# The scores of even and odd dilated heads, issued together on the two row halves of TensorE

## The reference, cut to what matters

```python
s = jnp.einsum('gnqhd,gnkhd->gnhqk', qs, kk).astype(jnp.float32) * (dh ** -0.5)
s = jnp.where(valid[None, :, None], s, NEG)
m = jnp.max(s, axis=-1, keepdims=True)
e = jnp.exp(s - m)
den = jnp.sum(e, axis=-1, keepdims=True)
o = jnp.einsum('gnhqk,gnkhd->gnqhd', (e / den).astype(v.dtype), vv)
```

## Time and profile before

| | |
|---|---|
| median of 3 runs | 2309.15 us (2308.07 to 2310.26) |
| the profiled execution | 2309.35 us, span of its instructions 2308.0 us |
| block two | from about 1300 us to the end |
| the two attention loops | about 1481 to 1529 us, and 2018 to 2063 us |

### The profile page before, as it was taken

The page is one execution under the profiler, slowest core; times in us unless marked ns, Lnnn a source line. Parts: engine busy times, 40 slices in busy tenths (PEclk is TensorE's granted clock), DMA queues, the critical chain, the costliest instruction groups (busy, mean ns, idle before and its releaser), DMA issues.

```text
span 2308.0 us, 28941 instructions
## 1 busy us (share of the span) xinstructions
PE 1955.2 (85%) x12336; PEld 1357.2 (59%) x12336; DVE 983.3 (43%) x1219; ACT 669.7 (29%) x812; POOL 66.9 (3%) x144
## 2 busy tenths in 40 slices
PE   7999999655666655666679999999999999999998
PEld 4768872111111111111136999779998999788997
DVE  3744661000000000000005657876658656876656
ACT  3433430000000000000004445564445444455444
POOL 0000000000000000000001001010001000100000
PEclk8999999778777787877799999999999999999999
DMA  7345899999999999999997554335554554424552
GB/s 307 120 173 206 321 371 426 429 433 429 433 430 432 431 431 429 433 428 433 429 405 297 192 206 153 133 137 183 192 183 164 190 194 174 152 90 176 195 193 87
DMA packets 53489, 647.44 MB, mean 281 GB/s; under 512 B 5936, under 2 KB 6448, under 8 KB 10096
## 3 DMA queue, kind: packets, MB, share of 16 engines
q1 hardware_dynamic: 53360, 645.59, 69.9%
HBM read 644.52 MB, written 1.05 MB: 280 GB/s over the span
## 4 chain that ended last, share of the span: by engine, by line
PE 59%; DMA 30%; DVE 6%; ACT 2%; issue 1%; POOL 1%; SPq 0%; DVEq 0%; ACTq 0%; POOLq 0%
DMA wide_b<-in_experts 29%; PE PS L490 14%; PE PS L492 13%; PE PS L491 13%; PE PS L948 4%; PE PS L983 4%; DVE low L1887 1%; PE PS L508 1%; PE PS L739 1%; PE PS L926 1%; PE PS L642 1%; PE PS L756 1%; PE PS L1260 1%; DMA ring<-in_wmod 1%; DVE XR L1951 1%
## 5 line engine op out<-in xcount | busy, mean ns | idle before, releaser
L1887 DVE TENSOR_TENSOR low<-ring,WH 128x2048 fp32r<-128x2048 f32 (+1 forms) x163 | 372.0, 2282 | 182.0 <-ACT WH L2276 179.4
L490 PE MATMUL PS<-XH,WH 128*128 128x256 f32 x1408 | 396.9, 282 | 3.2 <-DVE XL L1919 3.1
L491 PE MATMUL PS<-XL,WH 128*128 128x256 f32 x1408 | 395.2, 281 | 0.0
L492 PE MATMUL PS<-XH,low 128*128 128x256 f32 x1408 | 393.1, 279 | 0.0
L2276 ACT ACTIVATE WH<-ring 128x2048 fp32r<-128x2048 f32 (+1 forms) x164 | 313.1, 1909 | 28.1 <-PE PS L983 16.5
L490 PEld LDWEIGHTS PS<-XH,WH 128*128 128x128 f32 x1408 | 264.5, 188 | 6.7 <-issue 5.0
L492 PEld LDWEIGHTS PS<-XH,low 128*128 128x128 f32 x1408 | 267.4, 190 | 0.0
L491 PEld LDWEIGHTS PS<-XL,WH 128*128 128x128 f32 x1408 | 264.6, 188 | 1.4
L1869 DVE TENSOR_TENSOR T1S<-T1S,PS 128x512 f32<-128x512 f32 x16 | 11.0, 688 | 546.6 <-PE PS L948 546.6
L948 PE MATMUL PS<-ring,big 128*32 128x512 f32 x936 | 137.9, 740 | 52.3 <-DMA ring<-in_experts 52.3
L2544 ACT ACTIVATE T1S<-PS 128x512 f32<-128x512 f32 x16 | 9.6, 597 | 539.9 <-PE PS L948 539.9
(11 more groups left out here) (445 smaller groups left out, 2845.6 us busy)
## 6 DMA issues: line engine op xcount, KB each, us to landing
wide_b<-in_experts SPq DMA_DIRECT2D x30, 4096.0 KB, 23.7
wide_a<-in_experts SPq DMA_DIRECT2D x29, 4096.0 KB, 23.7
ring<-in_experts SPq DMA_DIRECT2D x28, 4096.0 KB, 24.0
ring<-in_fg SPq DMA_DIRECT2D x44, 1024.0 KB, 4.9
ring<-in_fu SPq DMA_DIRECT2D x44, 1024.0 KB, 4.9
ring<-in_fd SPq DMA_DIRECT2D x44, 1024.0 KB, 4.8
ring<-in_wmod SPq DMA_DIRECT2D x24, 1024.0 KB, 6.6
ring<-in_wgt SPq DMA_DIRECT2D x12, 1024.0 KB, 9.1
```

The costliest lines, as they stand in the source:

```text
L490: t.matmul(o, l[0], r[0], start=start, stop=False, skip_group_check=True)
L491: t.matmul(o, l[0], r[1], start=False, stop=False, skip_group_check=True)
L492: return t.matmul(o, l[1], r[0], start=False, stop=stop, skip_group_check=True)
L1887: own(v.tensor_tensor(low[:, w.slot.index, 0:size], w.flat, WH[:, w.slot.index, 0:size].bitcast(f32), ALU.subtract).then_inc(*c.wl.up()), ...
```

## The change

The six dilated groups of a layer are issued as three pairs by a new function `dilated_scores(g)`: it takes both score banks, and issues the matmuls of the even head (rows 0 to 63 of the array, bank 0) and of the odd head (rows 64 to 127, bank 1) in turn, head for head. So that the two groups of a pair hold neighbouring heads, the list of groups for the second 128 queries goes from heads (0, 2), (4, 6), (1, 3), (5, 7) to (0, 2), (1, 3), (4, 6), (5, 7). The pairs stand in steps 5, 7 and 9 of TensorE's loop; before, the six groups stood in steps 4 to 9. The programs of the other engines keep their text.

```diff
         groups = [(hs, m, 512 // len(hs), o) for o in (4, 6)
-                  for hs, m in [([0, 2, 4, 6], 0), ([1, 3, 5, 7], 0)] + [([h, h + 2], 1) for h in (0, 4, 1, 5)]]
+                  for hs, m in [([0, 2, 4, 6], 0), ([1, 3, 5, 7], 0)] + [([h, h + 2], 1) for h in (0, 1, 4, 5)]]
...
-                    if g == 6:
-                        P.wait_ge(c.dqv, 2 * l + 2)
-                        P.wait_ge(c.dqa, 2 * l + 2)
                     for i, h in enumerate(hs):
-                        if g < 6:
-                            q, k = QT2[0:96, h, m * 128:m * 128 + 128], KT[0:96, h, 0:w]
-                        else:
-                            s = slice(64 * (h % 2), 64 * (h % 2) + 64)
-                            q, k = DT[s, 0, h // 2, m * 128:m * 128 + 128], DT[s, 1, h // 2, 0:w]
-                        x = t.matmul(PS[:, b, i * w:i * w + w], q, k, start=True, stop=True)
+                        x = t.matmul(PS[:, b, i * w:i * w + w], QT2[0:96, h, m * 128:m * 128 + 128], KT[0:96, h, 0:w],
+                                     start=True, stop=True)
...
+                def dilated_scores(g):
+
+                    m, w = groups[g][1:3]
+                    take(0)
+                    take(1)
+                    if g == 6:
+                        P.wait_ge(c.dqv, 2 * l + 2)
+                        P.wait_ge(c.dqa, 2 * l + 2)
+                    n = len(groups[g][0])
+                    for i in range(n):
+                        for b in range(2):
+                            h = groups[g + b][0][i]
+                            s = slice(64 * b, 64 * b + 64)
+                            x = t.matmul(PS[:, b, i * w:i * w + w], DT[s, 0, h // 2, m * 128:m * 128 + 128],
+                                         DT[s, 1, h // 2, 0:w], start=True, stop=True)
+                            if i == n - 1:
+                                x.then_inc(*c.sc.up())
+                                held[b] = [(c.am, 12 * l + g + b + 1)]
...
                 for g in range(13):
-                    if g < 10:
+                    if g < 4:
                         scores(g + 2)
+                    if g in (5, 7, 9):
+                        dilated_scores(g + 1)
```

More of the change, by code:

```diff
@@ L1227, in scores @@
                         P.wait_ge(c.qta, 4 * l + 8)
+                    for i, h in enumerate(hs):
+                        x = t.matmul(PS[:, b, i * w:i * w + w], QT2[0:96, h, m * 128:m * 128 + 128], KT[0:96, h, 0:w],
+                                     start=True, stop=True)
+                    x.then_inc(*c.sc.up())
+                    held[b] = [(c.am, 12 * l + g + 1)]
+                def dilated_scores(g):
+                    m, w = groups[g][1:3]
+                    take(0)
+                    take(1)
                     if g == 6:
@@ L1230, in scores @@
                         P.wait_ge(c.dqa, 2 * l + 2)
-                    for i, h in enumerate(hs):
-                        if g < 6:
-                            q, k = QT2[0:96, h, m * 128:m * 128 + 128], KT[0:96, h, 0:w]
-                        else:
-                            s = slice(64 * (h % 2), 64 * (h % 2) + 64)
-                            q, k = DT[s, 0, h // 2, m * 128:m * 128 + 128], DT[s, 1, h // 2, 0:w]
-                        x = t.matmul(PS[:, b, i * w:i * w + w], q, k, start=True, stop=True)
-                    x.then_inc(*c.sc.up())
-                    held[b] = [(c.am, 12 * l + g + 1)]
+                    n = len(groups[g][0])
[6 more added lines that the diff above has]
+                            if i == n - 1:
+                                x.then_inc(*c.sc.up())
+                                held[b] = [(c.am, 12 * l + g + b + 1)]
                 def turns(g):
```

## The result

The change makes the kernel slower: 2336.36 us (median of 4, 2333.74 to 2338.05) against 2308.61 us for the kernel before; ratio 1.0117, 95% interval 1.0105 to 1.0129. That is 27 us. Run once more beside other kernels it was 1.0113 (1.0098 to 1.0128), 26 us.

The account below looks back on a forecast made before the run. TensorE is busiest, but VectorE's in-order queue, with under 5 us of slack, was taken to bound the loop once pairs come late. 2309.2 us + 18.0 for waits + 3 for the clock = 2330 us; range 2318 to 2341.

Parts of the forecast that it names:

- Steps 4 and 6 save nothing: TensorE's loop: `values(3)` and `values(5)` wait for VectorE's copies with or without scores issued ahead, so nothing is saved.
- The price of a pair: TensorE, steps 5, 7 and 9: 1.9 us for width 128, 1.3 us for width 256; bounds one burst to about two.
- full overlap: Case of row halves running wholly side by side: about 8.0 us lost a layer, 16 us for both.
- The rival that the halves don't overlap: Pairs in the loop: 10.4 us lost a layer, 2330 us, up to 2338 with clock loss; chance 0.86 together with the forecast.
- The walk: Step-by-step sum of delays through steps 5 to 11 of the loop: 9.0 us lost a layer, 18.0 for both.
- The clock: TensorE's granted clock falling behind its standstills: 1.5 us a layer, 3 us for both, bounds 0 to 8.
- first standstill: TensorE in step 6, before `values(5)`, waiting for VectorE's copy of `turns(5)`: about 4 us.
- second standstill: TensorE in step 7, before the first slice of `w_out`, waiting for VectorE's `low_rows`: over 2 us.
- last standstill: TensorE in step 10, before `values(9)`, waiting for VectorE's copy of `turns(9)`: some 3 us.
- Only the first standstill counts: Rival: ScalarE or VectorE catches up in steps 7 to 9, leaving 2.6 us a layer, 2314 us; chance 0.07.
- TensorE's saving shows: Rival: VectorE's copy is not late, so saved TensorE time shows: 2.5 up to 6.6 us, 2303 to 2307 us; chance 0.04.
- No change: Rival: VectorE's late steps and the saved matmuls cancel within 4.6 us; chance 0.03.

Follow-up runs that it names:

- late, kept apart: Changed kernel with each pair's even group first, one unused full-height identity matmul, then the odd group: 2336.07 us, ratio 1.0115.
- The fillings: Changed kernel with unused identity matmuls at the three standstills of TensorE in each layer: 2326.38 us, ratio 1.0079.
- the first set of runs: The changed kernel's first runs against the kernel before: 2336.36 us, ratio 1.0117; its second set, on another chip, gave 2333.96 us, ratio 1.0113.
- the last pair alone: Changed kernel with only the pair of groups 10 and 11 late (step 9), the others in steps 4 and 6: 2316.61 us, ratio 1.0033.
- early pairs and changed queues: Changed kernel with pairs in steps 4, 6 and 8 and work in VectorE's and ScalarE's queues reordered: 2303.53 us, ratio 0.9979.
- the early pairs: Changed kernel with the pairs issued one step earlier, in steps 4, 6 and 8: 2309.18 us, ratio 1.0008.
- the early pairs issued one group after the other: Changed kernel with pairs in steps 4, 6 and 8, all matmuls of one group before the other's: 2311.12 us, ratio 1.0014.
- only the first standstill filled: Changed kernel with 16 unused identity matmuls ahead of `values(5)` only: 2327.93 us, ratio 1.0086.

## Why the prediction was right, point by point

- **The direction and the place: right.** 2330 us was forecast, 2336 measured, inside the range of 2318 to 2341. VectorE idles 4.22 us before `masked(6)`, where over 4 were forecast; TensorE 4.08 before `values(5)` (some 4), 2.37 in step 7 (over 2), 2.90 before `values(9)` (some 3). That VectorE's order is the cause is shown by changing that order alone (half of the loss gone) and by moving the pairs back a step (all of it gone).
- **Steps 4 and 6 save nothing: right.** `values(3)` still starts 1.45 us behind the start of `turns(3)`, now with a wait of 0.85 us for the copy. Before it was 1.62, so a little, 0.2 us, was saved.
- **The price of a pair: mis-sized.** The prediction took 1.9 us for width 128, on the assumption that weight loads go one after the other, and 1.3 for width 256. Measured at full clock: 1.16 and 1.14 us, the price of one burst; the row halves overlap wholly, loads included. The first choice was the wrong end of its range. It put `masked(6)` 0.7 us too late; by the prediction's own bound for full overlap the waits are 16 us, not 18. The rival that the halves don't overlap is out, by these times and by "late, kept apart".
- **The walk: right.** It gives 8.0 us a layer for full overlap. With the clock held up by filling, the loops are 7.9 us longer in each layer. The medians, with 18.5 us for both, are coarser: their interval is 14.8 to 21.7.
- **The clock: mis-sized.** It was taken at 3 us, with bounds of 0 and 8. The fillings show 7.6 us by the medians, and in the traces the two loops are longer than with the fillings by 8.5 us (profile of the first set of runs) and 6.6 (of the second). The term counted only the 2.8 us of work behind the first standstill, and that at half its price. In windows of the trace PEclk is 0.50 from 1508 us on, through the second standstill, and 1.00 again from 1522 us. Beside the kernel with the fillings, layer one loses 2.2 us from `values(5)` to the first slice of `w_out`, where 1.4 were taken, and 2.5 from there to the pair of step 9, where nothing was: there `values(6)` and `turns(7)` take 1.80 and 1.06 us, and slices of `w_out` 0.63 instead of 0.39. The prediction put that stretch at nothing without giving a reason. A third fall behind the last standstill (PEclk 0.83 from 1530 to 1540 us) was foreseen as small.
- **Luck.** The two errors, 2 us too much for the pairs and some 4 to 5 too little for the clock, partly cancel; part of the nearness of 2330 to 2336 is owed to that.
- **The rivals.** "Only the first standstill counts": out, since the last pair alone costs 8.6 us. "TensorE's saving shows": out for this placing. It is real in the kernel with early pairs and changed queues, at 3.5 us for six pairs, far from the 6.6 of its upper bound. "No change" is out by the measured 27 us.

## What to carry to other kernels

Before an instruction that feeds another engine is moved one step later, read that engine's queue behind the instruction that waits for it: the delay is paid by all that stands there, less only its idle time up to the next handover (0.80 us here), and it comes back to the first engine through a copy that has nothing to do with the moved work. Make the idle time first, or move to an earlier step. And price a new standstill of TensorE with the clock behind it: here the waits cost 16 us by the traces (18 by the medians) and the clock 7 to 9.

## What the hardware showed that was not expected

- Two 64-row halves of the array, writing two banks, overlap wholly, weight loads included: 16 matmuls of 64x128 in 1.16 us where 8 take 1.16 in one half, and 8 of 64x256 in 1.14 us where 4 take 1.13.
- For width 256 the order did not matter: all matmuls of one half, then all of the other, took 1.14 us too; for width 128 it took 1.71 us. Only a full-height matmul between the halves parted them (2.53 to 2.6 us from the start to the next instruction).
- A single short wait can be enough for the granted clock to fall, but need not be. Around a wait of 1.55 us it was 0.77 over 4 us in layer one of the early pairs; around the same wait it stayed at 1.00 in layer two of that kernel and in both layers of the early pairs issued one group after the other. With only the first standstill filled, the one of 2.37 us was followed by a fall in layer one and by none in layer two. So a wait of this size can't be priced from its length alone. Before the change block two had waits of up to 1.2 us and stayed at 1.00 in the loops. At the lower level the eight matmuls of `values` take up to 1.97 us instead of 1.00 to 1.10.
